# Mixer feature projections: the normalised stream's high and low halves streamed as one 512-column operand

## The chip, the cores and the metric

The kernel runs on one core of a Trainium2 chip, in one launch. The metric is the device time of the whole program in microseconds (us).

## The reference, cut to what matters

Two transformer blocks over 256 tokens of width 1024. The part that the change touches is in the first block's mixer, which exists twice (two layers). With `u = rmsnorm(h) * g`:

```
proj = u @ w_in[l]                       # q_sb, k_sb, v_sb, q_fx, k_fx, v_fx, f_logit, q_mem
o_sb  = stick_breaking_attention(q_sb, k_sb, v_sb)     # 8 heads of 64
o_fx  = forgetting_attention(q_fx, k_fx, v_fx, log_f)  # 8 heads of 64
o_mem = memory_attention(q_mem, k_mem, v_mem)          # 4 heads of 128
gates = sigmoid(u @ w_gate[l] + b_gate[l])
```

Everything else (three SwiGLU or convolution feed-forward parts, the memory projections, a latent attention, the output norm) is unchanged.

## The kernel before, in words

Every large product is made of three: weights and activations are each split into a high part that TensorE's rounded fp32 format holds exactly and a low rest, and `high*high + high*low + low*high` is accumulated in PSUM. Weights come through a ring in chunks of at most 1024 columns. SyncE loads chunk n into one of 4 `raw` buffers as soon as VectorE has finished with chunk n-4. ScalarE copies it into the rounded format (`whi`, L553, called through `split_to`), VectorE subtracts to get `wlo` (L1072), both with 6 buffers, so ScalarE may split chunk n only when TensorE has used chunk n-6. The semaphores are `w_loaded`, `hi_ready`, `lo_ready`, `w_used`. The order of the work on every engine is written out by hand, and each engine takes its instructions strictly in that order.

The mixer of a layer handles its heads in four pairs (`NPAIR`), so the code around the change runs eight times. For a pair with first chunk `c`, TensorE runs:

- `feature_chunk(0)`: q_sb of the pair, transposed (128 features x 256 tokens), into bank 0; then the values product of the pair before (`sb_out`) and the memory scores into bank 6
- `feature_chunk(1)`: k_sb into bank 1; `feature_chunk(2)`: q_fx into bank 0, after VectorE has made `qs` of the first
- the stick-breaking scores (L1983, L1984), which wait for `ks` (`feat_done` at 4I+2); `feature_chunk(3)`: k_fx into bank 1; four transposes of the memory weights
- eight gate chunks of 384 columns, `gate_chunk(0, 0..3)` and `gate_chunk(1, 0..3)`, each for two token blocks t, in bank t. The first one waits, for t=0, until `qx` has been made of bank 0 and, for t=1, until `kx` has been made of bank 1 (`feat_done`). `gate_chunk(1, 0)` waits until VectorE has taken the first gates out of the same bank (`gate_done`, L1261)
- between them the forgetting scores, the memory values, the cumulative sums (L2017 and on), transposes and values.

A feature chunk is a call of `project`: for each of 8 slices k of the contraction three matmuls of 256 columns into the same half bank. The weights are the stationary operand here; the stream, `uhi` or `ulo`, is the moving one.

VectorE multiplies the four results by the tokens' `rstd` straight out of PSUM: `qs` (L1276), `ks` (L1283), `qx` (L1294, two halves of 64 partitions), `kx` (L1298, two halves). Between `ks` and `kx` stand the weight splits of chunks c+6, c+7 and the normalisation of the memory weights; behind `kx` stand the split of c+8, then `sb_sp`, `sb_w` (L1304, L1308), the forgetting scores (L1315), their maxima, the split of c+10, `fx_s`'s normalisation and the first gates (L1261). GpSimd masks `sb_sp` (L527) behind L1308, ScalarE rounds it (L732), GpSimd makes `sb_lo` (L529).

ScalarE's order in a pair is: the head outputs (L703) and the split of c+5, the memory exponentials (L715), the splits of c+6 and c+7, the absolute value of the stick-breaking scores (L721), their exponential (L723), the split of c+8, the logarithm (L726), `mem_pT` (L728), the splits of c+9 and c+10.

Of the kernel before, what the change touches and what calls it, by code (L numbers as in the profile page):

```python
# [14 lines left out]
P = 128  # L15
# [90 lines left out]
def program(nc, A, consts, out):  # L106
    ctx = ExitStack()
    with ctx:
# [12 lines left out]
        whi = [sb(f"whi{s}", [P, CW], F32R) for s in range(SLOTS)]  # L121
        wlo = [sb(f"wlo{s}", [P, CW], F32R) for s in range(SLOTS)]
        H = sb("H", [P, TT, DM])
        uhi, ulo = sb("uhi", [P, KT, TOK], F32R), sb("ulo", [P, KT, TOK], F32R)
        kmem = [sb(f"kmem{l}", [P, MH, TOK]) for l in range(LAYERS)]
        vmem = [sb(f"vmem{l}", [P, TT, MH * P]) for l in range(LAYERS)]
        par = sb("par", [P, PCOLS])
# [55 lines left out]
        with ExitStack() as o:  # L183
# [17 lines left out]
        rb = gates[:, 1, 2 * DM:2 * DM + TT * P].rearrange("p (t n) -> p t n", t=TT)  # L201
        qmem = gates[:, 1, 2 * DM:3 * DM].rearrange("p (h n) -> p h n", h=MH)
        fx_pT = sb_e
        features = [slice(0, HD), slice(HD, P)]
        c_rows = [slice(HD, HD + 8), slice(0, 8)]
        contracted = [slice(0, HD + 8), slice(0, P)]
# [51 lines left out]
            sem(n) for n in ("pT_full", "y_tap", "y_conv", "y_scaled", "yb_done", "yhi_done", "ylo_done"))  # L258
        kn_full = sem("kn_full")
        first_taken, first_tp = sem("first_taken"), sem("first_tp")  # L260
        tap_done, conv_done, silu_done, hid_done, chi_done, clo_done = (
            sem(n) for n in ("tap_done", "conv_done", "silu_done", "hid_done", "chi_done", "clo_done"))

        lat0_full, lat_sq, lat_root, lat_rec, lat_done = (
            sem(n) for n in ("lat0_full", "lat_sq", "lat_root", "lat_rec", "lat_done"))
# [32 lines left out]


        post = lambda b: b - 1  # L300
        acc = lambda b: 4 if b <= 6 else 0
        stat = lambda b, t, n: st[:, b * 20 + t * 10 + n:b * 20 + t * 10 + n + 1]
        SS, PB, PROOT, PREC, HS, HB, HROOT, RSTD = 0, 2, 3, 4, 5, 7, 8, 9
# [235 lines left out]
        def _(act):  # L539
# [125 lines left out]
            def mixer(l):  # L665
# [39 lines left out]
                for p in range(NPAIR):  # L705
                    I = l * NPAIR + p
                    c = c_pair_[l] + 12 * p
                    if p > 0:
                        head_high(FOX, p - 1)
                    split_to(c - 1 + SLOTS)  # L710
                    if p > 0:
                        head_high(SB, p - 1)
                    act.wait_ge(mem_max, I + 1)
                    for q in range(TT):
                        act.activation(mem_p[:, q * TOK:(q + 1) * TOK], bank[6][:, q * TOK:(q + 1) * TOK], ACT.Exp,  # L715
                                       bias=mmax[:, q:q + 1], accum_out=msum[:, q:q + 1]).then_inc(mem_exp, 1)
                    split_to(c + 1 + SLOTS)

                    act.wait_ge(sbz_full, I + 1)
                    for h in range(2):  # L720
                        act.activation(sb_e[:, h, :], bank[2 + h][:, 0:CAUSAL], ACT.Abs).then_inc(sb_act, 1)  # L721
                    act.wait_ge(sb_act, I * 4 + 2)
                    act.activation(sb_e[:, :, :], sb_e[:, :, :], ACT.Exp, scale=-1.0).then_inc(sb_act, 1)  # L723
                    split_to(c + 2 + SLOTS)
                    act.wait_ge(sb_act, I * 4 + 3)
                    act.activation(sb_e[:, :, :], sb_e[:, :, :], ACT.Ln, bias=1.0).then_inc(sb_act, 1)  # L726
                    act.wait_ge(mem_tp, I + 1)
                    act.activation(mem_pT[:, :], bank[7][:, :], ACT.Copy).then_inc(mem_pt, 1)  # L728
                    split_to(c + 4 + SLOTS)

                    act.wait_ge(sb_masked, I + 1)
                    act.activation(sb_hi[:, :, :], sb_sp[:, :, :], ACT.Copy).then_inc(sb_high, 1)  # L732
                    head_high(MEM, p)
                    act.wait_ge(fx_max, I * 2 + 2)
                    for h in range(2):
                        for q, (a, e) in enumerate(((0, P), (P, CAUSAL))):
                            n = 2 * q + h
                            act.activation(fx_s[:, h, a:e], fx_s[:, h, a:e], ACT.Exp, bias=fmax[:, n:n + 1],
                                           accum_out=fsum[:, n:n + 1]).then_inc(fx_exp, 1)
                    split_to(c + 8 + SLOTS)  # L740
# [110 lines left out]
            def conv_ffn(use):  # L851
# [26 lines left out]
                def newest_tap(f):  # L878
                    if f < 2:
                        act.wait_ge(first_tp, 2 * use + f + 1)  # L880
                    else:
                        act.wait_ge(w_used, n0 + 2 * f + 2)
                    y = conv_y[f % 2]
                    for s in range(2):
                        at = taps + s * FT + f
                        act.activation(y[:, s * TOK:(s + 1) * TOK], bank[conv_bank(f)][:, s * TOK:(s + 1) * TOK], ACT.Copy,  # L886
                                       scale=par[:, at:at + 1]).then_inc(tap_done, 1)

                def silu(f):
                    act.wait_ge(conv_done, 4 * (use * FT + f) + 3)  # L890
                    act.activation(sgc[f % 2][:, :], conv_y[f % 2][:, 0:TOK], ACT.Silu).then_inc(silu_done, 1)

                def high(f):
# [170 lines left out]
        def _(dve):  # L1064
# [153 lines left out]
            def mixer(l):  # L1218
# [45 lines left out]
                for p in range(NPAIR):  # L1264
                    I = l * NPAIR + p
                    c = c_pair_[l] + 12 * p
                    if p > 0:
                        head_low(FOX, p - 1)
                    for h in range(2):
# [2 lines left out]
                                          ALU.mult).then_inc(c_pair, 1)  # L1272
                    split_to(c - 1 + SLOTS)

                    dve.wait_ge(w_used, c + 1)
                    dve.scalar_tensor_tensor(qs[:, :], bank[0][:, 0:TOK], SB_SCALE, rstd_bc[:, :], ALU.mult, ALU.mult).then_inc(feat_done, 1)  # L1276
                    if p > 0:
                        head_low(SB, p - 1)
                    dve.wait_ge(mem_full, I + 1)
                    dve.tensor_reduce(mmax[:, :], pair_bank(6), AX_X, ALU.max, negate=True).then_inc(mem_max, 1)  # L1280
                    split_to(c + SLOTS)
                    dve.wait_ge(w_used, c + 2)
                    dve.tensor_tensor(ks[:, :], bank[1][:, 0:TOK], rstd_bc[:, :], ALU.mult).then_inc(feat_done, 1)  # L1283
                    dve.wait_ge(mem_exp, I * 2 + 2)
                    dve.reciprocal(mrec[:, :], msum[:, :]).then_inc(mem_rec, 1)
                    dve.wait_ge(mem_rec, I + 1)
# [2 lines left out]
                                                mrec[:, q:q + 1], None, ALU.mult)  # L1289
                    ins.then_inc(mem_norm, 1)  # L1290
                    split_to(c + 1 + SLOTS)
                    dve.wait_ge(w_used, c + 3)
                    for h, f in enumerate(features):
                        ins = dve.scalar_tensor_tensor(qx[h][f, :], bank[0][f, 0:TOK], SB_SCALE, rstd_bc[f, :], ALU.mult, ALU.mult)  # L1294
                    ins.then_inc(feat_done, 1)
                    dve.wait_ge(w_used, c + 4)
                    for h, f in enumerate(features):
                        ins = dve.tensor_tensor(kx[h][f, :], bank[1][f, 0:TOK], rstd_bc[f, :], ALU.mult)  # L1298
                    ins.then_inc(feat_done, 1)
                    split_to(c + 2 + SLOTS)  # L1300

                    dve.wait_ge(sb_act, I * 4 + 4)
                    for h in range(2):
                        ins = dve.scalar_tensor_tensor(sb_sp[:, h, :], bank[2 + h][:, 0:CAUSAL], 0.0, sb_e[:, h, :], ALU.max, ALU.add)  # L1304
# [173 lines left out]
            def conv_ffn(use):  # L1478
# [21 lines left out]
                def older_taps(f):  # L1500
                    y = conv_y[f % 2]
                    i = use * FT + f
                    dve.wait_ge(tap_done, 2 * i + 2)
                    for back in (1, 2):
                        for s in range(2):
                            a = s * TOK
                            if back == 2:
                                dve.wait_ge(conv_done, 4 * i + s + 1)
                            at = taps + (2 - back) * 2 * FT + s * FT + f
                            dve.scalar_tensor_tensor(y[:, a + back:a + TOK], bank[conv_bank(f)][:, a:a + TOK - back], par[:, at:at + 1],  # L1510
                                                     y[:, a + back:a + TOK], ALU.mult, ALU.add).then_inc(conv_done, 1)

                def hidden(f):
                    i = use * FT + f
                    dve.wait_ge(silu_done, i + 1)
                    dve.wait_ge(conv_done, 4 * i + 4)
                    if f >= 2:
                        dve.wait_ge(clo_done, i - 1)
                    dve.tensor_tensor(hf[f % 2][:, :], conv_y[f % 2][:, TOK:2 * TOK], sgc[f % 2][:, :], ALU.mult).then_inc(hid_done, 1)
# [153 lines left out]
        def _(pe):  # L1673
# [10 lines left out]
            def project(dst, c, kts, xh, xl, width=P, at=0, ready=None, skip=False):  # L1684

                for k in range(kts):
# [4 lines left out]
                    pe.matmul(dst, wh, xh[:, k, :], start=(k == 0), stop=False, skip_group_check=skip)  # L1691
                    pe.matmul(dst, wh, xl[:, k, :], start=False, stop=False, skip_group_check=skip)  # L1692
                    ins = pe.matmul(dst, wl, xh[:, k, :], start=False, stop=(k == kts - 1), skip_group_check=skip)  # L1693
                return ins

            def turn(src, dst):
# [176 lines left out]
            def mixer(l):  # L1873
# [67 lines left out]
                for p in range(NPAIR):  # L1941
# [2 lines left out]

                    def feature_chunk(n):
                        start_chunk(c + n)
                        project(bank[n % 2][:, 0:TOK], c + n, KT, uhi, ulo).then_inc(w_used, 1)

                    def gate_chunk(x, i):
                        n = c + 4 + 4 * x + i  # L1950
# [175 lines left out]
            def conv_ffn(use, b, out_b):  # L2126
# [11 lines left out]
                            stream_turn(b, 1, j - 2)  # L2138
                for f in range(2, FT):
                    if f >= 4:  # L2140
                        pe.wait_ge(conv_done, 4 * (use * FT + f - 4) + 4)
                    else:
                        pe.wait_ge(first_taken, 2 * use + f - 1)
                    for s in range(2):
# [213 lines left out]
```

## Time and profile before

| | |
|---|---|
| median of 3 runs | 1869.18 us (1869.04 to 1869.72) |
| the profiled execution, its own time | 1869.25 us |
| its span, first to last instruction | 1867.4 us |
| TensorE matmuls busy | 1843.3 us, 99% of the span |
| TensorE weight loads busy (beside the matmuls) | 1623.2 us, 87% |
| VectorE busy | 1210.5 us, 65% |
| ScalarE busy | 1035.3 us, 55% |
| GpSimd busy | 98.8 us, 5% |
| granted TensorE clock | 1.0 all along |

The busy time of a matmul in the profile runs from its start to the end of its result, and matmuls overlap; how fast a stream of them goes is seen from start to start. The idle time of an engine is given in brackets with what ended it.

### The profile page before, as it was taken

The page shows a single profiled execution, that of the slowest core. Times are in us where ns is not written, and L with a number is a line of the kernel's source. Part 1 is how long each engine was busy: PE and PEld are TensorE (multiplying, and loading weights), DVE is VectorE, ACT ScalarE, POOL GpSimd, SP SyncE. Part 2 cuts the span into 40 slices and gives each one's busy share as a digit, 9 for nine tenths or more (in the row PEclk, how much of TensorE's full clock was granted, in tenths as well). Part 3 has the DMA queues.
Part 4 walks back from the last instruction along what each step waited for, and adds up shares of the span by engine and source line. Part 5 has one row for each costly group of instructions (what it writes and reads, how often), then busy time and mean ns, then how long its engine had stood idle before and what let it go on. Part 6 is the DMA issues. An engine that isn't in the chain of part 4 may idle for free.

```text
span 1867.4 us, 26977 instructions
## 1 busy us (share of the span) xinstructions
PE 1843.3 (99%) x10455; PEld 1623.2 (87%) x10455; DVE 1210.5 (65%) x1824; ACT 1035.3 (55%) x1680; POOL 98.8 (5%) x78
## 2 busy tenths in 40 slices
PE   8999999999999999999999999999999999899998
PEld 6888899998888888888999888888889998879997
DVE  5555657677765466545777776555768765758763
ACT  6545544556554455445555655445557655757653
POOL 0000001110000000000011100000002210001210
PEclk9999999999999999999999999999999999999999
DMA  7655575445576547654654547654757654637662
GB/s 259 218 181 180 160 206 166 139 147 184 164 226 186 191 150 229 189 188 139 187 175 139 186 144 234 181 191 148 213 148 215 186 190 131 190 102 203 191 194 102
DMA packets 353792, 333.83 MB, mean 179 GB/s; under 512 B 25338, under 2 KB 299392, under 8 KB 353664
## 3 DMA queue, kind: packets, MB, share of 16 engines
q1 hardware_dynamic: 353120, 331.58, 57.9%
q8 instruction: 83, 1.36, 0.3%
q10 hardware_dynamic: 544, 0.52, 0.1%
q14 instruction: 45, 0.37, 0.1%
HBM read 330.97 MB, written 1.05 MB: 178 GB/s over the span
## 4 chain that ended last, share of the span: by engine, by line
PE 90%; DVE 5%; ACT 2%; DMA 1%; issue 1%; SPq 0%; ACTq 0%; DVEq 0%
PE bank L1680 21%; PE bank L1682 21%; PE bank L1681 21%; PE bank L1691 7%; PE bank L1693 7%; PE bank L1692 7%; PE bank L1697 3%; DVE wlo L1072 2%; DMA raw<-in_w_in 1%; ACT whi L553 1%; DVE ulo L1120 1%; DVE bank L1363 0%; PE bank L1932 0%; ACT uhi L579 0%; PE bank L1971 0%
## 5 line engine op out<-in xcount | busy, mean ns | idle before, releaser
L1072 DVE TENSOR_TENSOR wlo<-raw,whi 128x1024 fp32r<-128x1024 f32 (+3 forms) x638 | 761.4, 1202 | 447.0 <-ACT whi L553 444.2
L553 ACT ACTIVATE whi<-raw 128x1024 fp32r<-128x1024 f32 (+3 forms) x638 | 648.3, 1025 | 498.4 <-PE bank L1682 403.3
L1680 PE MATMUL bank<-whi,uhi 128*128 128x512 f32 (+2 forms) x1232 | 471.7, 383 | 3.0 <-DVE wlo L1072 2.0
L1682 PE MATMUL bank<-wlo,uhi 128*128 128x512 f32 (+2 forms) x1232 | 459.9, 373 | 0.0
L1681 PE MATMUL bank<-whi,ulo 128*128 128x512 f32 (+2 forms) x1232 | 459.2, 373 | 0.0
L1691 PE MATMUL bank<-uhi,whi 128*128 128x256 f32 x1024 | 293.1, 286 | 0.2 <-DVE gates L1261 0.2
L1692 PE MATMUL bank<-ulo,whi 128*128 128x256 f32 x1024 | 289.7, 283 | 0.0
L1693 PE MATMUL bank<-uhi,wlo 128*128 128x256 f32 x1024 | 289.6, 283 | 0.0
L1680 PEld LDWEIGHTS bank<-whi,uhi 128*128 128x128 f32 x1232 | 231.7, 188 | 37.8 <-DVE wlo L1072 3.4
L1682 PEld LDWEIGHTS bank<-wlo,uhi 128*128 128x128 f32 x1232 | 231.4, 188 | 35.4
L1681 PEld LDWEIGHTS bank<-whi,ulo 128*128 128x128 f32 x1232 | 231.8, 188 | 32.8
L1680 PE MATMUL bank<-whi,hhi 128*128 128x512 f32 x560 | 219.7, 392 | 0.0
L1682 PE MATMUL bank<-wlo,hhi 128*128 128x512 f32 x560 | 218.1, 389 | 0.0
L1681 PE MATMUL bank<-whi,hlo 128*128 128x512 f32 x560 | 218.0, 389 | 0.0
L1691 PEld LDWEIGHTS bank<-uhi,whi 128*128 128x128 f32 x1024 | 196.3, 192 | 3.0 <-DVE gates L1261 1.3
L1692 PEld LDWEIGHTS bank<-ulo,whi 128*128 128x128 f32 x1024 | 196.3, 192 | 0.3
L1693 PEld LDWEIGHTS bank<-uhi,wlo 128*128 128x128 f32 x1024 | 196.3, 192 | 0.0
L1682 PEld LDWEIGHTS bank<-wlo,hhi 128*128 128x128 f32 x560 | 105.1, 188 | 22.1
L1681 PEld LDWEIGHTS bank<-whi,hlo 128*128 128x128 f32 x560 | 105.2, 188 | 21.2
L1680 PEld LDWEIGHTS bank<-whi,hhi 128*128 128x128 f32 x560 | 105.2, 188 | 21.2
L1510 DVE SCALAR_TENSOR_TENSOR conv_y<-bank,par,conv_y 128x254 f32<-128x254 f32 (+1 forms) x176 | 72.7, 475 | 41.4 <-ACT conv_y L886 40.6
L535 POOL TENSOR_TENSOR hlo<-hf,hhi 128x256 fp32r<-128x256 f32 x44 | 56.1, 1276 | 707.3 <-ACT hhi L895 707.3
(287 smaller groups left out, 1725.7 us busy)
## 6 DMA issues: line engine op xcount, KB each, us to landing
raw<-in_ffn_w_up SPq DMA_DIRECT2D x351, 256.0 KB, 3.6
raw<-in_ffn_w_down SPq DMA_DIRECT2D x264, 256.0 KB, 2.9
raw<-in_ffn_w_gate SPq DMA_DIRECT2D x175, 256.0 KB, 3.0
raw<-in_w_gate SPq DMA_DIRECT2D x128, 192.0 KB, 3.0
raw<-in_w_in SPq DMA_DIRECT2D x80, 256.0 KB, 3.4
raw<-in_a_w_in SPq DMA_DIRECT2D x48, 256.0 KB, 3.3
raw<-in_w_mem_kv SPq DMA_DIRECT2D x32, 256.0 KB, 3.4
raw<-in_w_out SPq DMA_DIRECT2D x32, 256.0 KB, 2.9
```

The lines of the kernel that those rows point to most:

```text
L535: pool.tensor_tensor(hlo[:, f, :], hf[f % 2][:, :], hhi[:, f, :].bitcast(F32), ALU.subtract).then_inc(clo_done, 1)
L553: act.activation(whi[n % SLOTS][:, 0:w], raw[n % RAW][:, 0:w], ACT.Copy).then_inc(hi_ready, 1)
L1072: dve.tensor_tensor(wlo[n % SLOTS][:, 0:w], raw[n % RAW][:, 0:w], whi[n % SLOTS][:, 0:w].bitcast(F32), ALU.subtract).then_inc(lo_ready, 1)
L1120: dve.scalar_tensor_tensor(ulo[:, k, ts[t]], src, par[:, g:g + 1], uhi[:, k, ts[t]].bitcast(F32), ALU.mult, ALU.subtract).then_inc(u_done, 1)
L1510: dve.scalar_tensor_tensor(y[:, a + back:a + TOK], bank[conv_bank(f)][:, a:a + TOK - back], par[:, at:at + 1], y[:, a + back:a + TOK], ALU ...
L1680: pe.matmul(dst, xh, wh, start=start, stop=False)
L1681: pe.matmul(dst, xl, wh, start=False, stop=False)
L1682: return pe.matmul(dst, xh, wl, start=False, stop=stop)
L1691: pe.matmul(dst, wh, xh[:, k, :], start=(k == 0), stop=False, skip_group_check=skip)
L1692: pe.matmul(dst, wh, xl[:, k, :], start=False, stop=False, skip_group_check=skip)
L1693: ins = pe.matmul(dst, wl, xh[:, k, :], start=False, stop=(k == kts - 1), skip_group_check=skip)
L1697: return pe.transpose(dst, src, ident)
```

## The change

`uhi` and `ulo` become the two halves of each slice of one tile `u2`, so that slice k of both is one operand of 512 columns. The feature chunks use a new `project_wide`: for each k one matmul of `whi` against all 512 columns into a whole bank, and one of `wlo` against `uhi` into its first half. So the first half holds high*high + low*high, the second half high*low. ScalarE copies the second half into SBUF (`feature`, which lies in the space of `sb_sp`), VectorE adds the first half to it, and the four multiplications read the sum from SBUF. VectorE waits for its own `kx` before it writes `sb_sp`. Two semaphores get new names and serve both places.

```
-        uhi, ulo = sb("uhi", [P, KT, TOK], F32R), sb("ulo", [P, KT, TOK], F32R)
+        u2 = sb("u2", [P, KT, 2 * TOK], F32R)
+        uhi, ulo = u2[:, :, 0:TOK], u2[:, :, TOK:2 * TOK]
+        feature = [sb_sp[:, n, 0:TOK] for n in range(2)]

 ScalarE, in each pair
+                    def low_half(n):
+                        act.wait_ge(w_used, c + n + 1)
+                        act.activation(feature[n % 2], bank[n % 2][:, TOK:2 * TOK], ACT.Copy).then_inc(evicted, 1)
+
                     if p > 0:
                         head_high(FOX, p - 1)
                     split_to(c - 1 + SLOTS)
+                    low_half(0)
                     if p > 0:
                         head_high(SB, p - 1)
                     act.wait_ge(mem_max, I + 1)
                     (two exponentials)
+                    low_half(1)
                     split_to(c + 1 + SLOTS)
+                    low_half(2)
                     act.wait_ge(sbz_full, I + 1)
                     (two absolute values, the exponential)
                     split_to(c + 2 + SLOTS)
                     (the logarithm)
+                    low_half(3)
                     act.wait_ge(mem_tp, I + 1)

 VectorE, in each pair
+                    def sum_halves(n):
+                        dve.wait_ge(evicted, 4 * I + n + 1)
+                        dve.tensor_tensor(feature[n % 2], bank[n % 2][:, 0:TOK], feature[n % 2], ALU.add).then_inc(sum_done, 1)
+                        dve.wait_ge(sum_done, 4 * I + n + 1)
-                    dve.wait_ge(w_used, c + 1)
-                    dve.scalar_tensor_tensor(qs[:, :], bank[0][:, 0:TOK], SB_SCALE, rstd_bc[:, :], ALU.mult, ALU.mult).then_inc(feat_done, 1)
+                    sum_halves(0)
+                    dve.scalar_tensor_tensor(qs[:, :], feature[0], SB_SCALE, rstd_bc[:, :], ALU.mult, ALU.mult).then_inc(feat_done, 1)
                     (ks, qx and kx in the same way, from feature[1], [0], [1])
                     split_to(c + 2 + SLOTS)
+                    dve.wait_ge(feat_done, 4 * I + 4)
                     dve.wait_ge(sb_act, I * 4 + 4)

 TensorE
+            def project_wide(dst, c):
+                for k in range(KT):
+                    s = slice(k * P, (k + 1) * P)
+                    wh, wl = whi[c % SLOTS][:, s], wlo[c % SLOTS][:, s]
+                    if k == KT - 1:
+                        pe.matmul(dst[:, 0:TOK], wl, uhi[:, k, :], start=False, stop=False)
+                    ins = pe.matmul(dst, wh, u2[:, k, :], start=(k == 0), stop=(k == KT - 1))
+                    if k < KT - 1:
+                        pe.matmul(dst[:, 0:TOK], wl, uhi[:, k, :], start=False, stop=False)
+                return ins
                     def feature_chunk(n):
                         start_chunk(c + n)
-                        project(bank[n % 2][:, 0:TOK], c + n, KT, uhi, ulo).then_inc(w_used, 1)
+                        project_wide(bank[n % 2][:, :], c + n).then_inc(w_used, 1)
```

## Rows read from the trace of the kernel before

**Rows 1.** The page: busy time by engine, and the chain that ended last.
```profile
PE 1843.3 (99%) x10455; PEld 1623.2 (87%) x10455; DVE 1210.5 (65%) x1824; ACT 1035.3 (55%) x1680; POOL 98.8 (5%) x78
...
PE 90%; DVE 5%; ACT 2%; DMA 1%; issue 1%; SPq 0%; ACTq 0%; DVEq 0%
```

**Rows 2.** Waits of TensorE's matmuls: total us, times, longest.
```profile
PE bank L1691 <- DVE gates L1261: 0.2, 1, 0.2
```

**Rows 3.** Timeline of TensorE: start, us; a 512-column and a 256-column stretch.
```profile
77.29 0.40 PE L1681 MATMUL bank<-whi,ulo 128*128 128x512 f32 x1
...
87.76 0.39 PE L1682 MATMUL bank<-wlo,uhi 128*128 128x512 f32 x1
...
325.92 0.28 PE L1692 MATMUL bank<-ulo,whi 128*128 128x256 f32 x1
...
331.43 0.28 PE L1693 MATMUL bank<-uhi,wlo 128*128 128x256 f32 x1
```

**Rows 4.** Groups of VectorE instructions by line: count, busy us, mean ns, idle before.
```profile
L1519 DVE TENSOR_TENSOR hf<-conv_y,sgc 128x256 f32<-128x256 f32 x44 | 18.4, 419 | 0.4
...
L1249 DVE TENSOR_TENSOR olo<-bank,ohi 128x256 fp32r<-128x256 f32 x24 | 10.0, 418 | 5.0 <-ACT ohi L703 4.9
...
L1298 DVE TENSOR_TENSOR kx<-bank,rstd_bc 64x256 f32<-64x256 f32 x16 | 6.8, 422 | 24.6 <-PE bank L1693 24.5
```

**Rows 5.** Timeline of ScalarE in the second pair of the first layer.
```profile
321.09 0.39 ACT L703 ACTIVATE ohi<-bank 128x256 fp32r<-128x256 f32 x1 [1.43 <-PE bank L1933]
321.37 0.84 ACT L553 ACTIVATE whi<-raw 128x768 fp32r<-128x768 f32 x1
...
327.64 0.84 ACT L553 ACTIVATE whi<-raw 128x768 fp32r<-128x768 f32 x1
328.93 0.85 ACT L553 ACTIVATE whi<-raw 128x768 fp32r<-128x768 f32 x1 [0.45 <-PE bank L1693]
...
334.28 0.83 ACT L553 ACTIVATE whi<-raw 128x768 fp32r<-128x768 f32 x1
335.01 0.83 ACT L726 ACTIVATE sb_e<-sb_e 128x768 f32<-128x768 f32 x1
...
338.27 0.84 ACT L553 ACTIVATE whi<-raw 128x768 fp32r<-128x768 f32 x1 [0.83 <-PE bank L1682]
```

**Rows 6.** Timeline of VectorE in the same pair.
```profile
328.51 0.96 DVE L1072 TENSOR_TENSOR wlo<-raw,whi 128x768 fp32r<-128x768 f32 x1 [1.82 <-ACT whi L553]
329.39 0.42 DVE L1283 TENSOR_TENSOR ks<-bank,rstd_bc 128x256 f32<-128x256 f32 x1
...
335.67 0.86 DVE L1298 TENSOR_TENSOR kx<-bank,rstd_bc 64x256 f32<-64x256 f32 x2 [3.07 <-PE bank L1693]
...
342.76 2.49 DVE L1072 TENSOR_TENSOR wlo<-raw,whi 128x768 fp32r<-128x768 f32 x1
...
346.63 0.61 DVE L1261 SCALAR_TENSOR_TENSOR gates<-bank,st,gbias 128x384 f32<-128x384 f32 x1
```

**Rows 7.** Timeline of TensorE in the same pair, at the hand-overs.
```profile
328.55 0.28 PE L1693 MATMUL bank<-uhi,wlo 128*128 128x256 f32 x1
...
331.64 0.71 PE L1983 MATMUL bank<-qs,ks 64*128 64x256 f32 x4
...
335.35 0.28 PE L1693 MATMUL bank<-uhi,wlo 128*128 128x256 f32 x1
...
336.98 0.33 PE L1680 MATMUL bank<-whi,uhi 128*128 128x384 f32 x1
...
347.40 0.40 PE L1680 MATMUL bank<-whi,uhi 128*128 128x384 f32 x1
```

**Rows 8.** Timeline of GpSimd in the same pair.
```profile
342.60 1.84 POOL L529 TENSOR_TENSOR sb_lo<-sb_sp,sb_hi 128x768 fp32r<-128x768 f32 x1 [0.95 <-ACT sb_hi L732]
```

**Rows 9.** Timeline at the start of that pair: VectorE, and a weight load that waited.
```profile
320.26 0.62 DVE L1261 SCALAR_TENSOR_TENSOR gates<-bank,st,gbias 128x384 f32<-128x384 f32 x1 [0.36 <-PE bank L1682]
...
320.96 0.19 PEld L1691 LDWEIGHTS bank<-uhi,whi 128*128 128x128 f32 x1 [0.17 <-DVE gates L1261]
```

More of the change, by code:

```diff
@@ L260, in program @@
         first_taken, first_tp = sem("first_taken"), sem("first_tp")
-        tap_done, conv_done, silu_done, hid_done, chi_done, clo_done = (
-            sem(n) for n in ("tap_done", "conv_done", "silu_done", "hid_done", "chi_done", "clo_done"))
+        evicted, sum_done, silu_done, hid_done, chi_done, clo_done = (
+            sem(n) for n in ("evicted", "sum_done", "silu_done", "hid_done", "chi_done", "clo_done"))
         lat0_full, lat_sq, lat_root, lat_rec, lat_done = (
@@ L300, in program @@
         post = lambda b: b - 1
+        FEATS = LAYERS * NPAIR * 4
         acc = lambda b: 4 if b <= 6 else 0
@@ L886, in newest_tap @@
                         act.activation(y[:, s * TOK:(s + 1) * TOK], bank[conv_bank(f)][:, s * TOK:(s + 1) * TOK], ACT.Copy,
-                                       scale=par[:, at:at + 1]).then_inc(tap_done, 1)
+                                       scale=par[:, at:at + 1]).then_inc(evicted, 1)
                 def silu(f):
-                    act.wait_ge(conv_done, 4 * (use * FT + f) + 3)
+                    act.wait_ge(sum_done, FEATS + 4 * (use * FT + f) + 3)
                     act.activation(sgc[f % 2][:, :], conv_y[f % 2][:, 0:TOK], ACT.Silu).then_inc(silu_done, 1)
@@ L1281, in mixer @@
                     split_to(c + SLOTS)
-                    dve.wait_ge(w_used, c + 2)
-                    dve.tensor_tensor(ks[:, :], bank[1][:, 0:TOK], rstd_bc[:, :], ALU.mult).then_inc(feat_done, 1)
+                    sum_halves(1)
+                    dve.tensor_tensor(ks[:, :], feature[1], rstd_bc[:, :], ALU.mult).then_inc(feat_done, 1)
                     dve.wait_ge(mem_exp, I * 2 + 2)
@@ L1291, in mixer @@
                     split_to(c + 1 + SLOTS)
-                    dve.wait_ge(w_used, c + 3)
+                    sum_halves(2)
                     for h, f in enumerate(features):
-                        ins = dve.scalar_tensor_tensor(qx[h][f, :], bank[0][f, 0:TOK], SB_SCALE, rstd_bc[f, :], ALU.mult, ALU.mult)
+                        ins = dve.scalar_tensor_tensor(qx[h][f, :], feature[0][f, :], SB_SCALE, rstd_bc[f, :], ALU.mult, ALU.mult)
                     ins.then_inc(feat_done, 1)
-                    dve.wait_ge(w_used, c + 4)
+                    sum_halves(3)
                     for h, f in enumerate(features):
-                        ins = dve.tensor_tensor(kx[h][f, :], bank[1][f, 0:TOK], rstd_bc[f, :], ALU.mult)
+                        ins = dve.tensor_tensor(kx[h][f, :], feature[1][f, :], rstd_bc[f, :], ALU.mult)
                     ins.then_inc(feat_done, 1)
                     split_to(c + 2 + SLOTS)
+                    dve.wait_ge(feat_done, 4 * I + 4)
                     dve.wait_ge(sb_act, I * 4 + 4)
@@ L1502, in older_taps @@
                     i = use * FT + f
-                    dve.wait_ge(tap_done, 2 * i + 2)
+                    dve.wait_ge(evicted, FEATS + 2 * i + 2)
                     for back in (1, 2):
@@ L1507, in older_taps @@
                             if back == 2:
-                                dve.wait_ge(conv_done, 4 * i + s + 1)
+                                dve.wait_ge(sum_done, FEATS + 4 * i + s + 1)
                             at = taps + (2 - back) * 2 * FT + s * FT + f
                             dve.scalar_tensor_tensor(y[:, a + back:a + TOK], bank[conv_bank(f)][:, a:a + TOK - back], par[:, at:at + 1],
-                                                     y[:, a + back:a + TOK], ALU.mult, ALU.add).then_inc(conv_done, 1)
+                                                     y[:, a + back:a + TOK], ALU.mult, ALU.add).then_inc(sum_done, 1)
                 def hidden(f):
@@ L1515, in hidden @@
                     dve.wait_ge(silu_done, i + 1)
-                    dve.wait_ge(conv_done, 4 * i + 4)
+                    dve.wait_ge(sum_done, FEATS + 4 * i + 4)
                     if f >= 2:
@@ L2140, in conv_ffn @@
                     if f >= 4:
-                        pe.wait_ge(conv_done, 4 * (use * FT + f - 4) + 4)
+                        pe.wait_ge(sum_done, FEATS + 4 * (use * FT + f - 4) + 4)
                     else:
```

## The prediction

> **What bounds the kernel now.** I read the page first. TensorE is busy for 99% of the span and makes up 90% of the chain that ended last [rows 1]. So a microsecond taken from TensorE's stream is a microsecond of the kernel, and a wait put into it is one too. The waits come next: in the eight pairs of the mixer TensorE's matmuls wait for next to nothing, the only entry of the feature code being 0.2 us in all [rows 2]. The pairs run dense, so what counts is how much earlier than needed each hand-over from VectorE is ready. That is read in the timeline of one pair. I take the second pair of the first layer; the other pairs have the same offsets, as the group of `kx` shows: 16 instructions, 24.5 us of waiting for TensorE, 3.06 us in each of eight pairs [rows 4, 6].
>
> **What TensorE saves.** The 46 starts from 77.29 to 87.76 give 0.2276 us for a 512-column matmul; the 46 from 325.92 to 331.43 give 0.1198 us for a 256-column one [rows 3]. A chunk now takes 24 x 0.1198 = 2.88 us. With 8 wide and 8 narrow matmuls it takes 8 x (0.2276 + 0.1198) = 2.78 us. That is 0.10 us a chunk, 0.4 us a pair, 3.1 to 3.2 us for 32 chunks. The columns streamed are the same; what goes is the fixed part of 8 matmuls, about 12 ns each. No row shows wide and narrow ones in turn, so I bound it. If a wide one only costs what two narrow ones do, nothing is saved. If it lost its fixed part altogether (0.1078 us for the 256 columns between the two forms, twice: 0.2156 us), a chunk would save 0.19 us. I take 0.10, the rows of both forms themselves.
>
> The Trainium skill says in "TensorE: Matmul & The Clock Gate", Back-to-back issue gap, that an isolated gap is the columns at full clock plus 2.5 ns. By that rule merging two matmuls saves only 2.5 ns, 0.6 us in all for 256 merges; the rows have about 12 ns, so the page would make the case for this change weaker still. The sum goes by the rows.
>
> **What stands between a chunk and its multiplication.** Before: VectorE starts 0.04 us after the last result (335.35 + 0.28 = 335.63, then 335.67 [rows 6, 7]). After: ScalarE copies (0.39 us, as 128x256 out of PSUM in rows 5; it starts about 0.09 us after TensorE: 328.55 + 0.28 = 328.83, then 328.93 [rows 5, 7]), VectorE follows 0.04 us later, adds for 0.42 us (the same shape out of PSUM and SBUF, 418 ns), waits 0.04 us for itself, and multiplies for 0.42 us (two SBUF operands, 419 ns) or 0.86 us for two halves [rows 4, 6]. So every feature is ready 0.9 us later at least. Where is that hidden, and where not?
>
> *qs* has all of chunk 1 and the memory scores as cover. Hidden. Its 0.8 us delay VectorE where it had been waiting.
>
> *ks.* The copy of chunk 1 stands ahead of the split of c+6 on ScalarE, and it waits for TensorE to be done with chunk 1. That is the second cost of the order: the split of c+6 started at 327.64 [rows 5] and must now wait until 328.83 - 0.20 (two shorter chunks) = 328.63, + 0.09, + 0.28 (from start to start behind a copy of this size, 321.09 to 321.37 [rows 5]) = 329.00. VectorE's order has the low split of c+6 ahead of `ks`: it starts 0.03 us after the high one ends, 329.87, and the next instruction 0.88 us after its start (328.51 to 329.39 [rows 6]): the sum at 330.75, `ks` at 331.21, done at 331.63. TensorE sees a VectorE result 0.08 us later (320.26 + 0.62, then 320.96 [rows 9]): 331.71. It would come to its scores at 331.64 - 0.30 = 331.34 [rows 7]. It waits 0.37 us; its shift against the kernel before is then +0.07.
>
> *qx* is ready long before the gates. Hidden.
>
> *kx.* Chunk 3 is done at 335.63 + 0.07 - 0.10 = 335.60. ScalarE's copy stands behind the logarithm, which moves with the scores to 335.08, and follows it by 0.73 us (334.28 to 335.01 [rows 5]): 335.81. Then 336.20, the sum at 336.24, `kx` at 336.70, done at 337.56, seen by TensorE at 337.64. The second token block of the first gate chunk would start at 336.98 + 0.07 - 0.10 = 336.95 [rows 7]. It waits 0.69 us. A stream that was stopped starts again without a loaded weight, which costs about 0.09 us (347.40 is followed by its next matmul after 0.23 us, 336.98 by its own after 0.17). TensorE's shift: +0.75.
>
> *What is late next.* VectorE had no gap between `kx` and the first gates; everything behind `kx` on it is now 337.56 - 336.53 = 1.03 us late: the split of c+8, `sb_sp`, `sb_w`, the forgetting scores, the normalisation. GpSimd and ScalarE follow it. The split of c+10 took 2.49 us instead of 0.95, because it stood still until GpSimd's `sb_lo` (342.60 to 344.44) was over [rows 6, 8]; both hang on `sb_w`, so they move together and this keeps its length. The first gates then end at 346.63 + 0.61 + 1.03 = 348.27, seen at 348.35, and with 0.05 us of weight load the second half of the gates can start at 348.40. TensorE would be there at 347.40 + 0.75 = 348.15 [rows 6, 7]. Another 0.25 us, final shift +1.00. The rest of the pair has cover: the second gates are taken behind a wait for TensorE.
>
> The Trainium skill, "SBUF — State Buffer", Who interferes with whom, says that a VectorE instruction with two SBUF inputs and a GpSimd one that reads SBUF exclude each other; the trace agrees, with those 2.49 us. It would speak against the change where GpSimd runs beside the new multiplications. Here GpSimd is idle from one pair's last mask to the next `sb_w`, so it adds nothing to the sum.
>
> **Sum.** Eight pairs x 1.00 us = +8.0 us, in which the 3.1 us saved are already counted. The profiled execution took 1869.25 us in all (1867.4 of span and 1.9 around it), against a median of 1869.18. 1869.2 + 8.0 = 1877.2, I say 1877.2.
>
> ScalarE's 32 copies (32 x 0.39 = 12.5 us) and VectorE's 32 additions (13.4 us) cost nothing by their sum, since both have over a third of the time free; they cost by where they stand. Loads: the buffer of chunk c+6 is free 1.37 us later, but the split of c+10 waits for TensorE and not for the load [rows 5], and it has from 330.8 to 338.3. Hidden. The longer live time of `sb_sp` costs nothing: its own next writer comes behind `kx` anyway. The new layout of `u2` keeps every operand's columns side by side, so I cost it at nothing.
>
> **Rivals.**
> - *Everything is hidden* (0.07). Then TensorE's saving stands alone: 1869.2 - 3.1 = 1866.1, within 0.2%; with the fixed part gone altogether, 32 x 0.19 = 6.1, 1863.1, which is faster. It is decided at `kx`: 336.53 + 0.08 against 336.98 leaves 0.37 us of cover, and the copy by itself takes 0.39. For it speaks only the uncertainty of modelled matmul ends; the chain is over twice the cover.
> - *Only a small net loss* (0.11): the wide form saves its upper bound and the first gates overtake, say because the split of c+10 comes ahead of GpSimd's `sb_lo` (0.16 us apart now) and so takes 0.95 instead of 2.49. Then only the wait for `kx` is left: 0.69 + 0.09 - 0.4 or so, 0.4 us a pair, +3.2 us, 1872.4.
> - *The delays pile up* (0.12). Each new hand-over could take 0.09 instead of 0.04 us, three of them in the chain of `kx`, and the copy 0.47 instead of 0.39. Nothing saved by the wide form makes 1.2 us a pair; with these 1.45: 11.6, 1880.8. A gate chunk that then waits for a split, or GpSimd's instruction caught by a VectorE split, would bring 1.5 us a pair more, 1889.
> - *The forecast* (0.70): waits for `ks`, `kx` and the first gates, 0.8 us a pair (the wide form at its best, 6.5 us) to 1.2 us (nothing saved, 9.8 us): 1875.7 to 1879.0.
>
> **The numbers.** Within about 0.2%, 3.7 us, a measurement of this kernel can't tell a change. Slower by more: forecast, pile-up and nearly half of the small loss, 0.87. Within: the other half and most of the first rival, 0.10. Faster: 0.03. The range takes in the forecast's bounds, the upper bound of the hand-overs and the small loss: 1872.3 to 1881.5.
>
> **What would show it.** In the profile after: the starts of a wide and a narrow matmul 0.35 us apart in sum and chunks of 2.78 us; waits of L1983's successor for `ks`, of the gate's L1680 for `kx` and of L1680 for the gates, eight times each, about 0.4, 0.7 and 0.25 us; the pairs' period, 36.4 us, grown by 1.0. VectorE's instructions behind `kx` late by 1.0 against the start of the pair. The prediction is wrong if ScalarE's copy starts well before the logarithm's end, if the waits are missing, or if the wide matmuls lie at another distance.

## The result, and the profile after

Median 1876.24 us (7 runs, 1875.24 to 1876.91) against 1869.08 us before (7 runs): a ratio of 1.0036, 95% interval 1.0027 to 1.0046, which is 5.0 to 8.6 us. The change makes the kernel 7.2 us slower. The forecast was 8.0 us more, 1877.2.

The page of the changed kernel, busy time and chain:

```profile
PE 1845.6 (98%) x10199; PEld 1608.4 (86%) x10199; DVE 1222.1 (65%) x1856; ACT 1044.0 (56%) x1712; POOL 98.8 (5%) x78
...
PE 88%; DVE 5%; ACT 4%; issue 2%; DMA 1%; SPq 0%; ACTq 0%; DVEq 0%
```

There are 256 matmuls fewer, and TensorE's part of the chain went from 90% to 88% [rows 1]. Where it waits now is told by the weight loads' waits (total us, times, longest):

```profile
PEld bank L1699 <- DVE kx L1316: 6.0, 8, 0.8
...
PEld bank L1963 <- issue: 4.3, 16, 0.4
PEld bank L2014 <- DVE ks L1301: 4.0, 8, 0.5
...
PEld bank L1699 <- issue: 3.4, 12, 0.9
```

There are eight waits for `kx` and eight for `ks`. The third one forecast, for the first gates, has no entry under that name. But ahead of L1699, the first matmul of a gate chunk's slice, the idling that the profile calls "issue" has grown: the kernel before has 2.1 us in 4 times at that place, here it is 3.4 us in 12, eight more of about 0.16 us each. So the wait must be looked for at its place, in the same pair of the first layer. TensorE in the changed kernel (start, us):

```profile
321.82 0.50 PE L1722 MATMUL bank<-u,whi 128*128 128x512 f32 x1
...
325.65 0.70 PE L2002 MATMUL bank<-kmem,gates 128*128 128x256 f32 x2
...
326.97 0.40 PE L1722 MATMUL bank<-u,whi 128*128 128x512 f32 x1
327.20 0.28 PE L1724 MATMUL bank<-u,wlo 128*128 128x256 f32 x1
327.32 0.40 PE L1722 MATMUL bank<-u,whi 128*128 128x512 f32 x1
...
332.03 0.39 PE L1722 MATMUL bank<-u,whi 128*128 128x512 f32 x1
...
336.16 0.39 PE L1722 MATMUL bank<-u,whi 128*128 128x512 f32 x1
...
338.47 0.44 PE L1699 MATMUL bank<-whi,u 128*128 128x384 f32 x1 [0.44 <-DVE kx L1316]
338.75 0.34 PE L1700 MATMUL bank<-whi,u 128*128 128x384 f32 x1
...
348.89 0.28 PE L2052 MATMUL bank<-sb_lo,exact_r 128*128 128x256 f32 x1
349.16 0.41 PE L1699 MATMUL bank<-whi,u 128*128 128x384 f32 x1
...
362.99 0.70 PE L2002 MATMUL bank<-kmem,gates 128*128 128x256 f32 x2
```

Two weight loads of the same kernel, for the scores and for the first matmul of `gate_chunk(1, 0)`:

```profile
332.60 0.31 PEld L2014 LDWEIGHTS bank<-qs,ks 64*128 64x128 f32 x4 [0.50 <-DVE ks L1301]
...
349.13 0.19 PEld L1699 LDWEIGHTS bank<-whi,u 128*128 128x128 f32 x1 [0.17 <-issue]
```

ScalarE:

```profile
329.65 0.38 ACT L714 ACTIVATE sb_sp<-bank 128x256 f32<-128x256 f32 x1 [1.08 <-PE bank L1722]
329.93 0.84 ACT L556 ACTIVATE whi<-raw 128x768 fp32r<-128x768 f32 x1
...
335.98 0.83 ACT L737 ACTIVATE sb_e<-sb_e 128x768 f32<-128x768 f32 x1
336.71 0.36 ACT L714 ACTIVATE sb_sp<-bank 128x256 f32<-128x256 f32 x1
```

VectorE:

```profile
330.80 0.96 DVE L1084 TENSOR_TENSOR wlo<-raw,whi 128x768 fp32r<-128x768 f32 x1 [3.29 <-ACT whi L556]
331.67 0.42 DVE L1282 TENSOR_TENSOR sb_sp<-bank,sb_sp 128x256 f32<-128x256 f32 x1
332.12 0.42 DVE L1301 TENSOR_TENSOR ks<-sb_sp,rstd_bc 128x256 f32<-128x256 f32 x1
...
337.11 0.42 DVE L1282 TENSOR_TENSOR sb_sp<-bank,sb_sp 128x256 f32<-128x256 f32 x1 [1.74 <-ACT sb_sp L714]
337.57 0.85 DVE L1316 TENSOR_TENSOR kx<-sb_sp,rstd_bc 64x256 f32<-64x256 f32 x2
338.45 0.96 DVE L1084 TENSOR_TENSOR wlo<-raw,whi 128x768 fp32r<-128x768 f32 x1
339.33 1.01 DVE L1323 SCALAR_TENSOR_TENSOR sb_sp<-bank,sb_e 128x384 f32<-128x384 f32 x2
...
348.40 0.61 DVE L1273 SCALAR_TENSOR_TENSOR gates<-bank,st,gbias 128x384 f32<-128x384 f32 x1
```

This pair begins at 321.82; in the kernel before it began at 320.96 [rows 9]. With those 0.86 us taken off, the times compare with the forecast as follows:

| | before | forecast | measured |
|---|---|---|---|
| low split of c+6 starts | 328.51 | 329.87 | 329.94 |
| scores start | 331.64 | 331.71 | 331.74 |
| `kx` done | 336.53 | 337.56 | 337.56 |
| gate chunk, second token block | 336.98 | 337.64 | 337.61 |
| first gates done | 347.24 | 348.27 | 348.15 |
| `gate_chunk(1, 0)`, first matmul | 347.40 | about 348.4 | 348.30 |

The third wait is there, without a name: the matmul at 349.16 starts 0.27 us after the one ahead of it, where the kernel before has 0.12 (347.28 to 347.40), so it waits 0.15 us. The first gates end at 349.01 (348.40 + 0.61), and the weight load that needs their bank starts 0.12 us later.

A pair's length is the distance between the memory scores of two pairs (the L2002 rows above): 37.34 us, against 36.43 before (324.83 to 361.26). That is 0.91 us a pair, 7.3 us for eight, which is the whole result.

### The profile page after: what moved, and what is told of

The parts are those of the page before. It is cut to its first block, busy times and chain, and to the rows that moved or that the text cites. A ratio compares the mean times of both kernels' runs of the same rounds, so it can differ in the third digit from the quotient of the medians.

```text
span 1874.9 us, 26537 instructions
## 1 busy us (share of the span) xinstructions
PE 1845.6 (98%) x10199; PEld 1608.4 (86%) x10199; DVE 1222.1 (65%) x1856; ACT 1044.0 (56%) x1712; POOL 98.8 (5%) x78
## 4 chain that ended last, share of the span: by engine, by line
PE 88%; DVE 5%; ACT 4%; issue 2%; DMA 1%; SPq 0%; ACTq 0%; DVEq 0%
PE bank L1699 21%; PE bank L1701 21%; PE bank L1700 21%; PE bank L1710 5%; PE bank L1712 5%; PE bank L1711 5%; PE bank L1728 3%; DVE wlo L1084 2%; PE bank L1722 2%; ACT whi L556 1%; PE bank L1724 1%; DMA raw<-in_w_in 1%; DVE u L1132 1%; PE bank L1963 1%; DVE bank L1382 0%
## 5 line engine op out<-in xcount | busy, mean ns | idle before, releaser
L1699 PE MATMUL bank<-whi,u 128*128 128x512 f32 (+2 forms) x1232 | 472.4, 383 | 7.5 <-DVE kx L1316 3.5
L1701 PE MATMUL bank<-wlo,u 128*128 128x512 f32 (+2 forms) x1232 | 459.8, 373 | 0.0
L1700 PE MATMUL bank<-whi,u 128*128 128x512 f32 (+2 forms) x1232 | 458.9, 373 | 0.0
L1699 PEld LDWEIGHTS bank<-whi,u 128*128 128x128 f32 x1232 | 231.4, 188 | 46.1 <-DVE kx L1316 6.0
L1701 PEld LDWEIGHTS bank<-wlo,u 128*128 128x128 f32 x1232 | 231.2, 188 | 35.6
L1700 PEld LDWEIGHTS bank<-whi,u 128*128 128x128 f32 x1232 | 231.7, 188 | 32.7
L1699 PE MATMUL bank<-whi,hhi 128*128 128x512 f32 x560 | 219.7, 392 | 0.0
L1710 PE MATMUL bank<-u,whi 128*128 128x256 f32 x768 | 217.8, 284 | 0.0
L1712 PE MATMUL bank<-u,wlo 128*128 128x256 f32 x768 | 217.3, 283 | 0.0
L1711 PE MATMUL bank<-u,whi 128*128 128x256 f32 x768 | 217.3, 283 | 0.0
L1710 PEld LDWEIGHTS bank<-u,whi 128*128 128x128 f32 x768 | 147.4, 192 | 0.6 <-issue 0.4
L1711 PEld LDWEIGHTS bank<-u,whi 128*128 128x128 f32 x768 | 147.4, 192 | 0.1
L1712 PEld LDWEIGHTS bank<-u,wlo 128*128 128x128 f32 x768 | 147.4, 192 | 0.0
L1699 PEld LDWEIGHTS bank<-whi,hhi 128*128 128x128 f32 x560 | 105.1, 188 | 21.1
L1722 PE MATMUL bank<-u,whi 128*128 128x512 f32 x256 | 94.8, 409 | 0.0
```

The source lines that it names most:

```text
L1699: pe.matmul(dst, xh, wh, start=start, stop=False)
L1700: pe.matmul(dst, xl, wh, start=False, stop=False)
L1701: return pe.matmul(dst, xh, wl, start=False, stop=stop)
L1722: ins = pe.matmul(dst, wh, u2[:, k, :], start=(k == 0), stop=(k == KT - 1))
```

## The experiments

Each kernel is compared with the kernel before on the same chip. The length of the pair in the table runs from the memory scores of the second pair of the first layer to those of the third, as read in the profile of each.

| kernel | median us | before, us | ratio, 95% | pair, us |
|---|---|---|---|---|
| before | | | | 36.43 |
| changed | 1876.24 | 1869.08 | 1.0036 (1.0027 to 1.0046) | 37.34 |
| e1 wide alone | 1867.12 | 1869.38 | 0.9988 (0.9979 to 0.9996) | 36.23 |
| e2 hand-over alone | 1877.16 | 1869.38 | 1.0040 (1.0026 to 1.0054) | 37.43 |
| e3 split first | 1874.29 | 1869.38 | 1.0024 (1.0015 to 1.0034) | 37.08 |
| e4 banks free at the sum | 1877.43 | 1869.38 | 1.0042 (1.0029 to 1.0054) | 37.30 |
| e5 gates first | 1874.21 | 1869.14 | 1.0026 (1.0016 to 1.0037) | 37.09 |
| e6 e4 and e5 | 1871.08 | 1869.14 | 1.0011 (1.0002 to 1.0019) | 36.57 |
| e7 e3, e4 and e5 | 1868.71 | 1869.14 | 0.9999 (0.9990 to 1.0008) | 36.34 |
| e8 before, own wait | 1868.97 | 1869.14 | 0.9999 (0.9990 to 1.0008) | 36.45 |
| e9 e7, one wait less | 1868.42 | 1869.07 | 0.9998 (0.9989 to 1.0007) | 36.34 |
| e10 copy before the logarithm | 1875.42 | 1869.07 | 1.0034 (1.0022 to 1.0046) | 37.29 |
| e11 e9, `head_low(MEM)` first | 1866.97 | 1869.05 | 0.9990 (0.9981 to 0.9999) | 36.16 |
| e12 e1 again | 1867.67 | 1869.05 | 0.9991 (0.9982 to 1.0000) | 36.22 |

The intervals are some 3 us wide, more than most steps here. The length of this pair repeats to a few hundredths (before and e8, e1 and e12, e7 and e9), so the small steps are read from it, and the times decide on the whole. Single other pairs of a trace can be longer: 36.75 us once in the kernel before, 38.17 once in e2, 36.91 once in e11, where ScalarE had waited 1.83 us for a load of weights and TensorE then 0.47 us for ScalarE.

**The two halves of the change, each alone**

```
 e1
-                    low_half(0)      (and 1, 2, 3)
-                        dve.wait_ge(evicted, 4 * I + n + 1)
-                        dve.tensor_tensor(feature[n % 2], bank[n % 2][:, 0:TOK], feature[n % 2], ALU.add).then_inc(sum_done, 1)
-                        dve.wait_ge(sum_done, 4 * I + n + 1)
+                        dve.wait_ge(w_used, c + n + 1)
-  ... feature[0], SB_SCALE, rstd_bc[:, :], ...
+  ... bank[0][:, 0:TOK], SB_SCALE, rstd_bc[:, :], ...
```

> The wide matmuls alone: TensorE runs the feature chunks as in the changed kernel, but ScalarE copies nothing and VectorE multiplies the first half of the bank as before. Left out of the computation: the product of high weights and the stream's low half in q and k of the two attentions. Theory (the cost is the new hand-over, the matmuls themselves save time): faster than before by 32 chunks x 0.04 to 0.05 us, as the distance of 0.352 us from wide to wide in the changed kernel's trace has it against 3 x 0.120: about -1.5 us, 1867.6, and no wait for ks or kx. By the prediction's own term (0.10 us a chunk) -3.1 us, 1866.0. Rival (the wide form or the new layout itself costs): not faster than 1869.1.

```
 e2
-                    ins = pe.matmul(dst, wh, u2[:, k, :], start=(k == 0), stop=(k == KT - 1))
+                    pe.matmul(dst[:, 0:TOK], wh, uhi[:, k, :], start=(k == 0), stop=False, skip_group_check=True)
+                    pe.matmul(dst[:, TOK:2 * TOK], wh, ulo[:, k, :], start=False, stop=(k == KT - 1), skip_group_check=True)
                     (the third, low times high, into the first half)
```

> The hand-over alone: three 256-column matmuls per slice as before, but high times low goes to the second half of the bank, and ScalarE and VectorE do all that they do in the changed kernel. Theory: the waits for ks, kx and the first gates are all there; chunks are 0.05 us longer, of which the two on the way to kx count: +0.99 us a pair, +7.9 us, about 1877.0. Rival (the wide matmuls cost the time): back to about 1869.

Alone, the wide matmuls bring 2.3 us (0.8 to 3.9 by the interval), the hand-over alone costs 7.8 us. The pair of e1 is 0.20 us shorter than before, 0.05 us for each of its four chunks and 1.6 us in all. e12, the same kernel once more, has 36.22 us. The pair of e2 is 1.00 us longer than before. The time of e1 alone can't tell 1.5 from 3.1 us; by the length of the pair it is the smaller one. The rival, that the wide form or the layout costs anything, is out.

**One edit at a time on the changed kernel**

```
 e3, ScalarE
+                    split_to(c + SLOTS)
                     low_half(1)
                     split_to(c + 1 + SLOTS)
```

> The changed kernel with ScalarE's split of chunk c+6 ahead of its copy of the second feature chunk instead of behind it. Theory: the wait for ks, about 0.5 us at the weight load, is gone; the scores and with them the logarithm and the copy for kx come 0.2 us earlier, and everything behind kx too: +0.68 us a pair instead of 0.89, +5.4 us, 1874.5. Rival (the place on ScalarE does not count, only the longer chain): no change against 1876.2.

A pair is 0.26 us shorter than in the changed kernel (0.21 expected), and the time 4.9 us over before (5.4 expected). The wait for `ks` is gone from the weight loads' waits, that for `kx` stays at 6.0 us. The scores' weight load in e3:

```profile
332.38 0.31 PEld L2015 LDWEIGHTS bank<-qs,ks 64*128 64x128 f32 x4 [0.25 <-issue]
```

`ks` is done at 331.11 there, so 0.25 us of idling stand ahead of this load without any wait for it (e1 has the same 0.25). Of the 0.50 us in the changed kernel the wait for `ks` is thus the other 0.25, as much as the pair got shorter. The order on ScalarE, one instruction that had nothing to wait for put behind one that did, was over a quarter of the loss.

```
 e4, TensorE
-                                pe.wait_ge(feat_done, 4 * I + 3 + t)
+                                pe.wait_ge(sum_done, 4 * I + 3 + t)
+                    pe.wait_ge(feat_done, 4 * I + 4)          (ahead of the forgetting scores)
                     pe.wait_ge(c_pair, 2 * I + 2)
```

> The changed kernel, but the first gate chunk waits for the sums (the banks are read out then) and no longer for qx and kx; the forgetting scores, four matmul groups later, wait for kx. Theory (what counts is the latest wait; behind kx on VectorE stand the first gates, which stay as late): the wait of 0.75 us for kx goes and the wait for the first gates grows by as much: about 1876, no change against the changed kernel. Rival (the waits add up): 8 x 0.7 us less, about 1870.5.

```
 e5, VectorE
                     head_low(MEM, p)
+                    take_gate(p, 0)
                     (reciprocal and four multiplications of fx_s)
-                    take_gate(p, 0)
```

> The changed kernel, with VectorE taking the first gates ahead of the normalisation of the forgetting weights (four multiplications and a reciprocal, 1.1 us) instead of behind it. Theory: only the last of the three waits goes, TensorE's shift stays at the 0.75 us it has behind kx: +5.9 us, 1875.0. Rival (the gates are the bound as such): the whole 0.9 us a pair goes, about 1869.

> Both of the last two edits: banks free at the sums, and the gates ahead of the normalisation. Theory: the waits for kx and for the gates are both off the path; only the wait for ks is left, TensorE's shift is 0.05 us a pair: +0.4 us, 1869.5. Rival (each edit brings what it brings alone, added up): about 1874.5 to 1875.

These three show what is late next. e4 takes away the largest of the waits that the change brought, 6.0 us of weight-load idling, and gains nothing: 1877.43, a pair of 37.30 against 37.34. What happened is seen in the waits of TensorE's matmuls in e4:

```profile
PE bank L1699 <- DVE gates L1273: 4.1, 8, 0.5
...
PE bank L2014 <- DVE ks L1301: 1.5, 8, 0.2
```

The wait for the gates took the place of that for `kx`. e5 alone is worth 0.25 us a pair; its rival, that the gates are the bound as such, falls (1874.21, not 1869). Its pair, 37.09, is 0.09 us shorter than the 0.75 us of shift that were expected to stay would make it; most of that is a small wait for the gates that the kernel before has too, seen below. Together the two edits are worth 0.77: the pair goes to 36.57. Alone they give 0.04 and 0.25, so what they bring together is not the sum. The rival of e6 falls. But e6 was expected at 36.48 and 1869.5, and came 1.6 us above that, 0.1 us a pair: something was still waiting.

**All edits, and the wait without a name**

> All three edits: the split of c+6 ahead of the copy, banks free at the sums, gates ahead of the normalisation. Theory: none of the new waits is left, the saving of the wide matmuls stands alone: 32 x 0.047 = 1.5 us faster than before, 1867.6. Rival (another wait takes their place, for instance the copy engine's rounding or a load): 1869 or more.

> The kernel of e7 without TensorE's wait for c_pair ahead of the forgetting scores; VectorE raises it long before feat_done, for which TensorE waits at the same place. In e7 a pair takes 36.33 us against 36.43 before, 0.1 us more than the 36.23 of e1: up to the fourth gate chunk e7 keeps its lead of 0.19 us, and then it loses 0.13 us at the first cumulative-sum matmul, whose weight load idles 0.2 us for no wait that the trace shows. Theory A (one more waiting instruction in TensorE's stream is what shows there): 36.23 us, 0.8 us in all less than e7, 1867.5 to 1868. Theory B (it has another reason): 36.33 us, the time of e7.

e7 is level with before (0.9990 to 1.0008; a pair of 36.34 us), not 1.5 us ahead. Within the pair its lead of 0.19 us on the kernel before is there up to the fourth gate chunk and shrinks at the first cumulative sum. e9 took out one wait instruction ahead of the forgetting scores; the pair stayed at 36.34, so theory A falls. In e9 the weight load of the first cumulative sum idles, and VectorE ends an instruction just before it starts. The weight loads and VectorE of e9:

```profile
346.00 0.30 PEld L2049 LDWEIGHTS bank<-sb_hi,exact_r 128*128 128x128 f32 x2 [0.22 <-issue]
```

```profile
343.11 2.49 DVE L1085 TENSOR_TENSOR wlo<-raw,whi 128x768 fp32r<-128x768 f32 x1
345.52 0.41 DVE L1262 TENSOR_TENSOR olo<-bank,ohi 128x256 fp32r<-128x256 f32 x1
```

345.52 + 0.41 = 345.93, and 0.07 us later the load starts. TensorE waits there for `olo_done` of the memory head, whose instruction stands behind the split that GpSimd holds up. The profile calls that idling "issue". e11 tests this by moving the instruction:

```
 e11, VectorE
-                    split_to(c + 4 + SLOTS)
                     head_low(MEM, p)
+                    split_to(c + 4 + SLOTS)
```

> The kernel of e9, with VectorE's head_low(MEM) ahead of the split of chunk c+10 instead of behind it. In e9's trace the weight load of the first cumulative-sum matmul starts at 346.00 after 0.22 us of idling; VectorE's head_low(MEM), for which TensorE waits there, ends at 345.93, 0.07 us earlier: it stands behind the split that is held up by GpSimd. Theory (this is the one wait that is left): that idling goes and a pair takes 36.23 us, as in e1: 1867.5. The split itself still ends with GpSimd. Rival (TensorE's sequencer is what is late there, or the split moves into another GpSimd instruction and the gates come late): 36.33 us or more, the time of e9 or above.

> The kernel of e1 again, on the same chip as e11. Left out of the computation: the product of high weights and the stream's low half in q and k of the two attentions. If nothing of the hand-over is left on the path in e11, both take the same time and the same 36.23 us a pair.

VectorE in e11, where the head's low part comes first and the split is still held up by GpSimd's instruction (343.35 to 345.20), 2.10 us instead of 0.95:

```profile
343.57 0.42 DVE L1262 TENSOR_TENSOR olo<-bank,ohi 128x256 fp32r<-128x256 f32 x1
343.91 2.10 DVE L1085 TENSOR_TENSOR wlo<-raw,whi 128x768 fp32r<-128x768 f32 x1
```

The idling is gone, and the rival with it. e11 takes 1866.97 us, 0.9990 of before (0.9981 to 0.9999), 2.1 us less: by the edge of the interval it beats the kernel before, and clearly the changed one, by some 9 us. It still has all 32 copies and all 32 additions, and takes the time of e1 and e12, which have none: the work that the hand-over adds costs nothing that can be measured once it stands where nobody waits for it. Its pair is even 0.07 us shorter than that of e1, 36.16 against 36.23. The matmuls of the two run alike, hundredth for hundredth, up to the first matmul of `gate_chunk(1, 0)`, and part there. TensorE in e1 (two rows), then in e11:

```profile
346.80 0.41 PE L1687 MATMUL bank<-whi,u 128*128 128x384 f32 x1
347.05 0.34 PE L1688 MATMUL bank<-whi,u 128*128 128x384 f32 x1
```

```profile
347.30 0.34 PE L1700 MATMUL bank<-whi,u 128*128 128x384 f32 x1
347.48 0.34 PE L1701 MATMUL bank<-whi,u 128*128 128x384 f32 x1
```

To the next one it is 0.25 us in e1 (0.23 in the kernel before), 0.18 in e11, and 0.18 in e5 too, which takes the gates first and leaves all else as in the changed kernel. So the kernel before has a wait of 0.05 to 0.07 us for the first gates as well: they end there at 347.24 [rows 6], and the weight load behind them starts at 347.35. Taking the gates first removes it. e11's 0.27 us a pair are thus 0.20 of the wide matmuls and 0.07 of the gates.

**Two small ones**

```
 e8, on the kernel before, VectorE
+                    dve.wait_ge(feat_done, 4 * I + 4)
                     dve.wait_ge(sb_act, I * 4 + 4)
```

> The kernel before with one line of the change, VectorE's wait for its own kx ahead of sb_sp. In the changed kernel sb_sp started 0.88 us after the split ahead of it, against 0.99 us before, which is most of the 0.11 us a pair by which the prediction was too high. Theory A (the added wait brings this, whatever its reason): 0.88 us here too. Theory B (the reason is elsewhere, as in what sb_sp waits for): 0.99 us. The time stays at 1869.1 in both, since TensorE waits for nothing there.

```
 e10, ScalarE
+                    low_half(3)
                     act.activation(sb_e[:, :, :], sb_e[:, :, :], ACT.Ln, bias=1.0).then_inc(sb_act, 1)
-                    low_half(3)
```

> The changed kernel with ScalarE's copy of the fourth feature chunk ahead of the logarithm instead of behind it. In the changed kernel's trace the copy starts at 336.71, and chunk 3 is done at 336.55, so the order costs at most 0.07 us of the prediction's 0.13: kx starts at 337.50 instead of 337.57, 0.5 us in all, 1875.7; the logarithm is 0.95 us later and sb_sp does not wait for it. Rival (sb_sp then waits for the logarithm and the delay behind kx grows): slower than the changed kernel, up to 1878.

In e8 `sb_sp` starts 0.99 us after the split (336.64 to 337.63), as before; theory A falls. In e10 a pair is 0.05 us shorter and `kx` starts at 337.51, as expected; the later logarithm does not delay `sb_sp`, which starts 0.87 us after the split, as in the changed kernel (0.88), and the rival falls.

## Why the prediction was right, step by step

The terms of the sum, in us a pair, against what the traces show in the second pair:

| | forecast | measured |
|---|---|---|
| saving of the four wide chunks | -0.40 | -0.20 |
| wait for `ks` | +0.37 | +0.25 |
| wait for `kx` | +0.69 | +0.60 |
| start after that stop | +0.09 | +0.11 |
| wait for the first gates | +0.25 | +0.15 |
| sum | +1.00 | +0.91 |

- **What bounds, and where to look.** Right: the loss is where a result is now late, and it comes from engines that have a third of their time free.
- **The saving of the wide matmuls.** The mechanism is right, the size was twice too big. Wide and narrow together were put at 0.347 us; in turn they take 0.352 (from 326.97 on, wide to wide), which leaves 0.06 us a chunk, and a little more is lost at the ends of a chunk. The step is the term of 0.10 us a chunk; e1 measures 0.05, 1.6 us in all instead of 3.1. The bounds (0 and 0.19) held it. By the rule that the prediction cites from the Trainium skill, "TensorE: Matmul & The Clock Gate", Back-to-back issue gap, it would have been an estimated 0.6 us; the measured 1.6 decides.
- **Why that error hardly reached the sum.** Where VectorE's result sets the time, a TensorE that saves less comes later and waits less: it came 0.15 us later than forecast to the scores and 0.06 us later to the gates' second block, and the two waits are 0.12 and 0.09 us shorter. Only the saving of the two chunks ahead of `ks` counts, since they make the result itself earlier; all that these chunks really save is 0.09 us a pair (e2 against the changed kernel). There the sum had some luck: chunk 1 was done at 328.75 instead of 328.63 (329.21 + 0.40 - 0.86), but ScalarE's copy began 0.04 us behind it and not 0.09, and small differences in the steps that follow took off the rest, so that `kx` was done at 337.56, as forecast.
- **The chain behind a chunk.** Right within 0.03 us: copy 0.38 (0.39), hand-over, addition 0.42, 0.04, multiplication. 337.11 + 0.46 = 337.57 is the start of `kx`.
- **The wait for `ks`, by ScalarE's order.** The cause is right, as e3 shows. The size is 0.25 us, not 0.37: of the 0.50 us that the load idles, e1 and e3 have 0.25 without any wait for `ks`.
- **The wait for `kx`.** The time is right: 337.61 against 337.64. The wait itself is 0.60 us: the matmul ahead starts at 337.70, the next would follow 0.17 later and starts at 338.47. The prediction's 0.09 us for the start after a stop is not what its two figures give (0.23 - 0.17 = 0.06); measured are 0.28 - 0.17 = 0.11. The logarithm's share was put at 0.12 us behind the chunk and is at most 0.07 (e10: 0.05 us a pair).
- **The first gates late next.** Right in kind, and shown by e4 to be what sets the end. In size forecast 0.25 us, measured about 0.15: TensorE comes as forecast (348.15), but VectorE arrives there 0.91 instead of 1.03 us late, since `sb_sp` starts 0.88 us after the split ahead of it (338.45 to 339.33), not 0.99. That is the step behind the 0.1 us a pair by which the sum was too high. All kernels with the sums have 0.87 or 0.88, those without (before, e1, e8, e12) 0.99. It is not the added wait (e8); its reason is open, and no run isolates it.
- **GpSimd's hold on the split.** Right: the split of c+10 took 2.50 us again, no more.
- **Rivals.** Everything hidden: out, and it took four edits of orders and waits to get there (e11). Small net loss: out; its condition, a split of c+10 of 0.95 us, did not come true. Pile-up: out; VectorE's hand-overs kept their 0.04 us. (Its last figure, 1889, adds 1.5 us a pair to the forecast; added to the pile-up's own 1880.8 it would be 1892.8.)

## What to carry to other kernels

When an edit puts a step between two engines, do the sum of its busy time last. First walk the order on each engine that the step goes through, and for every instruction behind it that another engine waits for, compare the new time with the time of need. Removing the largest of the new waits can bring nothing if something further down the same queue is as late (e4); a set of edits is worth trying together, because here two that gave 0.04 and 0.25 us a pair alone gave 0.77 together. And an instruction with nothing to wait for should not stand behind one that waits, nor a short one that another engine needs behind a long one (e3, e5, e11).

## What the runs showed of the hardware that was not expected

- A wide and a narrow matmul in turn keep a distance of 0.352 us for 768 columns, where stretches of one form alone would give 0.2276 + 0.1198 = 0.347, and three narrow ones 0.359.
- Idling of a weight load that the profile puts down to "issue" can be a wait for VectorE (e9: the result 0.07 us before the load; e11: gone when that result comes earlier; changed kernel: 0.17 us ahead of the load at 349.13, gone in e5). It need not be: the 0.25 us ahead of the scores' load in e1 and e3 stand there though `ks` is done over 1 us earlier.
- On VectorE the first instruction of 128x384 behind the split of c+8 starts 0.99 us after it, or 0.88 in the kernels that have the sums, in all eight pairs; unexplained.
